# The order of sixteen matmuls per weight tile in a two-layer block with expert tables: interleaved, or in runs

## The chip, the cores and the metric

One core of a Trainium2 chip runs the whole program in one launch. The metric is the device time of that core in microseconds. The kernel before took 2291.82 us, the median of three runs (2289.64 to 2294.68).

## The reference, cut to what matters

The program is a retention and attention block with a feed-forward part, and after it two layers that each end in an expert layer over 16,384 experts. The change touches only products of 256 tokens with the weights of these expert layers:

```
def peer(h, wq, keys, u_tab, v_tab):                    # 256 tokens h, once in each of 2 layers
    q = (h @ wq)                                        # 1024 -> 2048: the queries
    s = einsum(q, keys)                                 # 128 keys per half
    ... top 16 of each half, top 16 of their sums: idx, gate = softmax(best)
    act = gelu(einsum('nd,nhkd->nhk', h, u_tab[idx]))   # the kernel forms h @ u_tab.T for all 16384
    return einsum('nhk,nhkd->nd', gate * act, v_tab[idx])
```

The reference gathers 16 rows of the tables for each token and head. The kernel computes the product with the whole first table (16,384 x 1024), and later multiplies the whole second table with a weight matrix that is zero where no expert was chosen.

## The kernel before, in words

**Numbers in two parts.** Weights come as 32-bit floats and are used at the matmul's reduced 32-bit format (fp32r). For accuracy each weight tile is split: `spl` is the rounded, high part, which ScalarE makes (L1097); `low` is what is left, `ring - spl`, which VectorE makes (L2600), or GpSimd for every second tile of the first 64 of the table (L2921, rule `lo_on_dve`). The tokens are split in the same way: `hT[:, 0]` is their high part, `hT[:, 1]` their low part. A product is then three: high by high, high weight by low token, low weight by high token.

**A weight tile.** Tiles have 128 x 1024 words, 512 KB. Five slots (`SLOTS`) hold the raw tile, its high and its low part. SyncE loads tile n when TensorE has told that it is done with tile n - 5 (`used`). ScalarE makes the high part two or three tiles ahead of its use, VectorE or GpSimd the low part behind it.

**The order written out by hand.** There is no scheduler: every engine has its own program, and semaphores with counted events join them. `hi.at(n)` is the event "the high part of tile n is there", `lo_at(n)` the same of the low part. `pe_take` waits for the low part, which is made from the high one, and so for both.

**Token-minor products.** In the expert layer 16 query tiles (`pe_peer`, loop over f) and 128 tiles of the first table (`pe_u`, 64 pairs) have the same form: 8 blocks k of 128 inputs. The stationary operand is a 128 x 128 piece of the weights. For the high part of the weights one matmul of 512 columns takes both parts of the tokens as moving operand (256 tokens high, 256 low, two pieces of `hT` that do not lie side by side) and fills one PSUM bank. For the low part one matmul of 256 columns takes the high tokens and adds to the first half of that bank. `mm3_both` writes these two for one block, wide then narrow; for the last block the narrow one goes first, so that the matmul that ends the group covers the whole bank. That makes 16 matmuls per tile, 16 + 128 tiles per layer, 288 tiles in both. The whole bank is read by ScalarE and VectorE when the tile (or the pair) is done.

**The first query tile.** The tokens' low part comes from VectorE in steps: events `("lo", k)`, where blocks 2 and 3, 4 and 5, 6 and 7 come in pairs from one instruction (L2447). Only the tile f = 0 waits for them, block by block.

**What stands between the tiles.** After f = 11 and f = 15 TensorE computes 32 small score products (L2804), after the pairs 14 and 30 of the table it transposes the chosen experts (L2815), and in the second half of the table each pair is preceded by 16 small matmuls that scatter the gates (`pe_scatter`, L2864). After that come 128 tiles of the second table (`pe_v`), with `mm3`: 12 matmuls of 512 columns per tile (L450 to L452), whose moving operand is the weight tile.

Of the kernel before, what the change touches and what calls it, by code (L numbers as in the profile page):

```python
# [174 lines left out]
U_BANK = (1, 4, 6)  # L175
# [254 lines left out]
def cut(p, f):  # L430
    return f(p[0]), f(p[1])
# [3 lines left out]
    return v[:, tb, c * 512:(c + 1) * 512]  # L435


def mm3_both(q, b, l, r, start, stop):


    if not stop:
        q.matmul(b[:, :].rearrange("p (z t) -> p z t", z=2), l[0], r, start=start, stop=False)  # L442
        return q.matmul(b[:, 0:256], l[1], r[:, 0], start=False, stop=False)  # L443
    q.matmul(b[:, 0:256], l[1], r[:, 0], start=False, stop=False)  # L444
    return q.matmul(b[:, :].rearrange("p (z t) -> p z t", z=2), l[0], r, start=False, stop=True)  # L445


def mm3(q, o, l, r, start, stop):
# [52 lines left out]
def pe_take(q, P, n):  # L501
    q.wait_ge(*P.lo_at(n))
    return P.tile(n)
# [1065 lines left out]
def ln_out(act, dve, tb, c):  # L1569

    return (act if c else dve).at(("ln", tb, c))
# [1202 lines left out]
def pe_peer(q, P, l):  # L2774
    T = T_PEER[l]
    b4act, b4dve = P.stage(("abo", "pool")[l])[1:]
    pe, act, dve = P.stage(f"peer{l}")
    if l == 0:
        first = [b4act.at(("turn", g)) for g in (4, 5, 2, 3)]
    else:  # L2780
        first = [b4dve.at(("mTf", 2)), b4dve.at(("mTf", 3)), b4act.at(("e", 5)), b4act.at(("e", 7))]
    pe_turns(q, P, pe, (0, 1, 2, 3),
             lambda k, tb: (P.xr[:, tb, k * 128:(k + 1) * 128], ln_out(b4act, b4dve, tb, k // 4)), first)
    for f in range(16):
        n = T + f
        sl = pe_take(q, P, n)
        if f == 0:
            q.wait_ge(*act.at(("turn", 3)))
        elif f == 2:
            q.wait_ge(*act.at(("turn", 7)))  # L2790
        elif f % 2 == 0:
            q.wait_ge(*dve.at(("q", f // 2 - 2)))
        for k in range(8):
            if f == 0:
                q.wait_ge(*dve.at(("lo", k)))
            t = mm3_both(q, P.ps[f % 4], cut(sl, lambda v: v[:, k * 128:(k + 1) * 128]), P.hT[:, :, k, :],
                         k == 0, k == 7)
        t.then_inc(*pe.mark(("used", n), *([("q", f // 2)] if f % 2 else [])))
        for tb, g0 in SC_AFTER.get(f, ()):
            q.wait_ge(*P.line(f"keys{g0 // 8}_loaded").at((l, g0 // 8)))  # L2800
            q.wait_ge(*dve.at(("q", g0 // 2 + 1)))
            q.wait_ge(*(act.at(("sc", tb, g0 - 8)) if g0 >= 8 else b4dve.at(("y", tb, g0 // 4))))
            for g in range(4):
                t = q.matmul(P.ps[4 + 2 * tb + g0 // 4 % 2][:, g * 128:(g + 1) * 128],  # L2804
                             P.qT[:, g0 + g, tb * 128:(tb + 1) * 128],
                             P.keys[:, (g0 + g) * 128:(g0 + g + 1) * 128], start=True, stop=True)
            t.then_inc(*pe.mark(("sc", tb, g0)))
    for p in range(32):
        pe_u(q, P, l, p)
        if p % 16 == 14:  # L2810
            tb = p // 16
            q.wait_ge(*dve.at(("gsoft", tb)))
            q.wait_ge(*(dve.at(("rtout", 0)) if tb else dve.at(("q", 6))))
            for z in range(3):
                t = q.transpose(P.ps[0][:, z * 128:(z + 1) * 128], P.ij[:, z, :], P.ident[:, :])  # L2815
            t.then_inc(*pe.mark(("rt", tb)))
    for r in range(32):
        pe_scatter(q, P, l, 0, r)
        pe_u(q, P, l, 32 + r)
    for r in range(32):  # L2820
        pe_scatter(q, P, l, 1, r)
        pe_v(q, P, l, 2 * r)
        pe_v(q, P, l, 2 * r + 1)
    for j in range(64, 125):
        pe_v(q, P, l, j)
        pe_fold(q, P, ("v", l, j))
    for tb in range(2):
        for c in range(2):
            for j in range(125, 128):
                pe_v(q, P, l, j, (tb,), (c,))  # L2830


def pe_u(q, P, l, p):

    pe, act, dve = P.stage(f"peer{l}")
    if p >= 3:
        q.wait_ge(*dve.at(("us", p - 3)))
    elif p:
        q.wait_ge(*act.at(("sc", p - 1, 12)))
    else:  # L2840
        q.wait_ge(*dve.at(("q", 7)))
    for d in range(2):
        n = T_PEER[l] + 16 + 2 * p + d
        sl = pe_take(q, P, n)
        for k in range(8):
            t = mm3_both(q, P.ps[U_BANK[p % 3] + d], cut(sl, lambda v: v[:, k * 128:(k + 1) * 128]),
                         P.hT[:, :, k, :], k == 0, k == 7)
        t.then_inc(*pe.mark(("used", n), *([("u", p)] if d else [])))


# [35 lines left out]
def pe_program(q, P):  # L2886
    pe_in(q, P)
    pe_wo(q, P)
    pe_up(q, P)
    pe_down(q, P)  # L2890
    pe_ab(q, P)
    pe_abo(q, P)
    pe_peer(q, P, 0)
    pe_pool(q, P)
    pe_peer(q, P, 1)
# [256 lines left out]
```

## Time and profile before

| | |
|---|---|
| median of three runs | 2291.82 us |
| the profiled execution | 2289.48 us, of which the span of the instructions is 2288.2 us |
| TensorE busy (matmuls) | 2237.6 us, 98% of the span |
| wide matmuls of the touched tiles, L442 | 2016, mean 401 ns |
| narrow matmuls of the touched tiles, L443 | 2016, mean 281 ns |
| VectorE, ScalarE, GpSimd busy | 82%, 52%, 7% |
| mean granted TensorE clock | 0.993 of full |

How to read it: matmuls are pipelined, and the time that the profile gives to one of them reaches from its start to the modelled arrival of its results, so that the times of neighbours overlap. What a matmul costs in a stream is the distance from its start to the start of the next one, and this is read from the times in the left column of the timeline. L444 and L445 are the two matmuls of the last block, narrow and wide; there are 288 of each.

### The profile page before, as it was taken

How to read it: one execution, taken by the hardware profiler on the slowest of the kernel's cores; microseconds unless marked ns; L12 is line 12 of the kernel's file. 1: busy time of each engine (PE TensorE's matmuls, PEld its weight loads, DVE VectorE, ACT ScalarE, POOL GpSimd, SP SyncE). 2: the span in 40 equal slices, each digit the busy share in tenths (PEclk: the TensorE clock that was granted, in tenths of full speed). 3: DMA queues.
4: the chain of work that ended last, by engine and by line, in shares of the span. 5: the costliest groups of instructions: out<-in, count | busy, mean ns of one | idle time of the engine just before them, and what ended most of it. 6: DMA issues, size and time to landing. Idle time of an engine off the chain costs nothing.

```text
span 2288.2 us, 34776 instructions
## 1 busy us (share of the span) xinstructions
PE 2237.6 (98%) x13446; PEld 1887.6 (82%) x13446; DVE 1868.9 (82%) x3365; ACT 1199.7 (52%) x1754; POOL 168.4 (7%) x75
## 2 busy tenths in 40 slices
PE   9999999999999999999999999899999999999997
PEld 7789978777888888888888877788888888887886
DVE  8679996568688988888888888869998888887656
ACT  7555554456456555554444445455665554444553
POOL 0000000000044400000000000014430000000000
PEclk9999999999999999999999999999999999999999
DMA  8366593233555555555558996455555555556674
GB/s 293 123 207 218 192 356 114 92 120 102 184 176 185 188 175 169 172 170 175 175 175 300 340 357 235 147 185 185 185 185 173 173 171 173 175 175 217 218 239 136
DMA packets 123508, 442.32 MB, mean 193 GB/s; under 512 B 13760, under 2 KB 16832, under 8 KB 122704
## 3 DMA queue, kind: packets, MB, share of 16 engines
q1 hardware_dynamic: 117464, 425.04, 56.4%
q10 hardware_dynamic: 5880, 15.06, 1.9%
q8 instruction: 108, 1.77, 0.3%
q14 instruction: 56, 0.46, 0.1%
HBM read 436.88 MB, written 3.16 MB: 192 GB/s over the span
## 4 chain that ended last, share of the span: by engine, by line
PE 82%; DVE 10%; ACT 3%; DMA 2%; issue 2%; SPq 0%; ACTq 0%; DVEq 0%
PE psum L442 21%; PE psum L450 13%; PE psum L452 13%; PE psum L451 13%; PE psum L443 10%; PE psum L445 3%; PE psum L2864 3%; DVE low L2600 3%; DVE acc L1777 2%; PE psum L444 1%; DVE cv L2108 1%; DMA ring<-in_peer_v 1%; ACT spl L1097 1%; ACT cv L1398 1%; PE psum L918 1%
## 5 line engine op out<-in xcount | busy, mean ns | idle before, releaser
L2600 DVE TENSOR_TENSOR low<-ring,spl 128x1024 fp32r<-128x1024 f32 x638 | 779.2, 1228 | 255.0 <-ACT spl L1097 253.4
L1097 ACT ACTIVATE spl<-ring 128x1024 fp32r<-128x1024 f32 x702 | 735.4, 1053 | 288.2 <-DMA ring<-in_peer_u 163.7
L442 PE MATMUL psum<-hT,spl 128*128 128x512 f32 x2016 | 730.7, 401 | 2.5 <-DVE hT L1757 2.5
L443 PE MATMUL psum<-hT,low 128*128 128x256 f32 x2016 | 566.5, 281 | 0.0
L442 PEld LDWEIGHTS psum<-hT,spl 128*128 128x128 f32 x2016 | 381.2, 189 | 81.2 <-issue 3.1
L450 PE MATMUL psum<-spl,Ws 128*128 128x512 f32 x1024 | 407.0, 398 | 7.0 <-DVE Ws L2638 7.0
L452 PE MATMUL psum<-spl,Ws 128*128 128x512 f32 x1024 | 399.6, 390 | 0.0
L451 PE MATMUL psum<-low,Ws 128*128 128x512 f32 x1024 | 398.3, 389 | 0.0
L443 PEld LDWEIGHTS psum<-hT,low 128*128 128x128 f32 x2016 | 382.8, 190 | 9.6
L1706 ACT ACTIVATE Ws<-S 128x256 fp32r<-128x256 f32 x256 | 106.6, 417 | 357.0 <-PE psum L452 352.4
L2921 POOL TENSOR_TENSOR low<-ring,spl 128x1024 fp32r<-128x1024 f32 x64 | 162.0, 2532 | 1135.6 <-ACT spl L1097 1135.6
L450 PEld LDWEIGHTS psum<-spl,Ws 128*128 128x128 f32 x1024 | 192.4, 188 | 47.5 <-DVE low L2600 9.0
L452 PEld LDWEIGHTS psum<-spl,Ws 128*128 128x128 f32 x1024 | 192.2, 188 | 41.6
L451 PEld LDWEIGHTS psum<-low,Ws 128*128 128x128 f32 x1024 | 192.6, 188 | 38.8 <-issue 0.7
L1689 ACT ACTIVATE S<-psum 128x512 f32<-128x512 f32 x128 | 76.5, 598 | 152.1 <-PE psum L445 151.9
L2633 DVE TENSOR_TENSOR S<-psum,S 128x512 f32<-128x512 f32 x128 | 87.7, 685 | 48.6 <-ACT S L1689 48.3
L450 PE MATMUL psum<-spl,hT 128*128 128x512 f32 (+1 forms) x284 | 115.4, 406 | 7.2 <-DVE low L2600 4.9
L445 PE MATMUL psum<-hT,spl 128*128 128x512 f32 x288 | 114.4, 397 | 0.0
L452 PE MATMUL psum<-spl,hT 128*128 128x512 f32 (+1 forms) x284 | 111.0, 391 | 0.0
L451 PE MATMUL psum<-low,hT 128*128 128x512 f32 (+1 forms) x284 | 110.7, 390 | 0.0
L2638 DVE TENSOR_TENSOR Ws<-S,Ws 128x256 fp32r<-128x256 f32 x256 | 106.6, 417 | 1.1 <-ACT Ws L1706 1.1
L450 PE MATMUL psum<-hT,spl 128*128 128x256 f32 x352 | 102.6, 291 | 3.8 <-DVE low L2600 2.1
(413 smaller groups left out, 3038.1 us busy)
## 6 DMA issues: line engine op xcount, KB each, us to landing
ring<-in_peer_u SPq DMA_DIRECT2D x256, 512.0 KB, 3.5
ring<-in_peer_v SPq DMA_DIRECT2D x256, 512.0 KB, 3.7
vring<-in_ada_w SPq DMA_DIRECT2D x56, 512.0 KB, 6.2
ring<-in_w_up SPq DMA_DIRECT2D x44, 512.0 KB, 5.2
aring<-in_ada_w SPq DMA_DIRECT2D x40, 512.0 KB, 5.2
ring<-in_ab_in SPq DMA_DIRECT2D x32, 512.0 KB, 3.5
ring<-in_peer_wq SPq DMA_DIRECT2D x32, 512.0 KB, 4.3
ring<-in_w_down SPq DMA_DIRECT2D x22, 512.0 KB, 5.9
```

Of the source, the lines that this page charges most:

```text
L442: q.matmul(b[:, :].rearrange("p (z t) -> p z t", z=2), l[0], r, start=start, stop=False)
L443: return q.matmul(b[:, 0:256], l[1], r[:, 0], start=False, stop=False)
L445: return q.matmul(b[:, :].rearrange("p (z t) -> p z t", z=2), l[0], r, start=False, stop=True)
L450: q.matmul(o, l[0], r[0], start=start, stop=False)
L451: q.matmul(o, l[0], r[1], start=False, stop=False)
L452: return q.matmul(o, l[1], r[0], start=False, stop=stop)
L1097: q.activation(P.spl[:, m % SLOTS, 0:w], P.ring[:, m % SLOTS, 0:w], ACT.Copy).then_inc(*P.hi.mark(m))
L1706: q.activation(P.Ws[:, j % 3, 0, :], P.S[:, j, :], ACT.Copy).then_inc(*act.mark(("ws", j)))
L2600: q.tensor_tensor(P.low[:, n % SLOTS, 0:w], P.ring[:, n % SLOTS, 0:w], P.spl[:, n % SLOTS, 0:w].bitcast(F32), ALU.subtract).then_inc(*P.lo ...
L2633: q.tensor_tensor(x, P.psum[:, b:b + 2, 0:256], x, ALU.add).then_inc(*dve.mark(("us", p)))
L2638: q.tensor_tensor(P.Ws[:, j % 3, 1, :], P.S[:, j, :], P.Ws[:, j % 3, 0, :].bitcast(F32), ALU.subtract).then_inc(*dve.mark(("ws", j)))
L2921: q.tensor_tensor(P.low[:, n % SLOTS, 0:w], P.ring[:, n % SLOTS, 0:w], P.spl[:, n % SLOTS, 0:w].bitcast(F32), ALU.subtract).then_inc(*P.lo ...
```

## The change

`mm3_both` goes. A new function, `pe_tokens`, writes a tile's sixteen matmuls: the wide ones of blocks 0 to 6, then the narrow ones of all eight blocks, then the wide one of block 7, which ends the group. At the tile's start it waits for the high part only, and for the low part ahead of the first narrow matmul. For f = 0 the waits for the tokens' low part stand ahead of the wide matmul of each block; the one of block 7 stands ahead of the narrow ones.

```diff
-def mm3_both(q, b, l, r, start, stop):
-    if not stop:
-        q.matmul(b[:, :].rearrange("p (z t) -> p z t", z=2), l[0], r, start=start, stop=False)
-        return q.matmul(b[:, 0:256], l[1], r[:, 0], start=False, stop=False)
-    q.matmul(b[:, 0:256], l[1], r[:, 0], start=False, stop=False)
-    return q.matmul(b[:, :].rearrange("p (z t) -> p z t", z=2), l[0], r, start=False, stop=True)
+def pe_tokens(q, P, b, n, x_hi):
+    hi, lo = P.tile(n)
+    w = lambda v, k: v[:, k * 128:(k + 1) * 128]
+    wide = b[:, :].rearrange("p (z t) -> p z t", z=2)
+    q.wait_ge(*P.hi.at(n))
+    for k in range(7):
+        x_hi(k)
+        q.matmul(wide, w(hi, k), P.hT[:, :, k, :], start=k == 0, stop=False)
+    x_hi(7)
+    q.wait_ge(*P.lo_at(n))
+    for k in range(8):
+        q.matmul(b[:, 0:256], w(lo, k), P.hT[:, 0, k, :], start=False, stop=False)
+    return q.matmul(wide, w(hi, 7), P.hT[:, :, 7, :], start=False, stop=True)
...
-        for k in range(8):
-            if f == 0:
-                q.wait_ge(*dve.at(("lo", k)))
-            t = mm3_both(q, P.ps[f % 4], cut(sl, lambda v: v[:, k * 128:(k + 1) * 128]), P.hT[:, :, k, :],
-                         k == 0, k == 7)
+        t = pe_tokens(q, P, P.ps[f % 4], n, lambda k: q.wait_ge(*dve.at(("lo", k))) if f == 0 else None)
...
-            t = mm3_both(q, P.ps[U_BANK[p % 3] + d], cut(sl, lambda v: v[:, k * 128:(k + 1) * 128]),
-                         P.hT[:, :, k, :], k == 0, k == 7)
+        t = pe_tokens(q, P, P.ps[U_BANK[p % 3] + d], n, lambda k: None)
```

TensorE's program around the border between two tiles of the first table, before (L442 and L445 wide, L443 and L444 narrow; `s_split_lo_pool` is GpSimd's event for a low part, `s_peer0_dve` the one by which VectorE gives a PSUM bank back):

```order
L442 MATMUL psum<-hT,spl 128x512
L443 MATMUL psum<-hT,low 128x256
L444 MATMUL psum<-hT,low 128x256
L445 MATMUL psum<-hT,spl 128x512
L442 MATMUL psum<-hT,spl 128x512 [waits s_split_lo_pool,s_peer0_dve]
L443 MATMUL psum<-hT,low 128x256
L442 MATMUL psum<-hT,spl 128x512
```

The same place of the changed kernel, a whole tile with its neighbours' ends (L447 and L452 wide, L451 narrow):

```order
L451 MATMUL psum<-hT,low 128x256 [waits s_split_lo_dve]
L451 MATMUL psum<-hT,low 128x256 x7
L452 MATMUL psum<-hT,spl 128x512
L447 MATMUL psum<-hT,spl 128x512 [waits s_split_hi,s_peer0_dve]
L447 MATMUL psum<-hT,spl 128x512 x6
L451 MATMUL psum<-hT,low 128x256 [waits s_split_lo_pool]
L451 MATMUL psum<-hT,low 128x256 x7
L452 MATMUL psum<-hT,spl 128x512
```

The narrow matmuls, which stood one by one behind the wide ones, now stand in one row of eight; the wide ones stand in a row of eight across the border of two tiles; and the wait for the low part has moved from the tile's first matmul to its eighth.

TensorE's program at the first query tile of layer 0, before:

```order
L442 MATMUL psum<-hT,spl 128x512 [waits s_peer0_dve,s_peer0_act,s_split_lo_dve]
L443 MATMUL psum<-hT,low 128x256
L442 MATMUL psum<-hT,spl 128x512 [waits s_peer0_dve]
L443 MATMUL psum<-hT,low 128x256
L442 MATMUL psum<-hT,spl 128x512 [waits s_peer0_dve]
```

And now:

```order
L447 MATMUL psum<-hT,spl 128x512 [waits s_peer0_dve,s_split_hi,s_peer0_act]
L447 MATMUL psum<-hT,spl 128x512 [waits s_peer0_dve] x6
L451 MATMUL psum<-hT,low 128x256 [waits s_split_lo_dve,s_peer0_dve]
L451 MATMUL psum<-hT,low 128x256 x7
```

Here `s_peer0_dve` is the event of the tokens' low part: the six waits of blocks 1 to 6 now follow each other at the distance of one wide matmul instead of a wide and a narrow one.

## Rows read from the trace of the kernel before

**Rows 1.** The page: engines (busy us, share, instructions) and the wide matmuls (busy, mean, idle before)
```profile
PE 2237.6 (98%) x13446; PEld 1887.6 (82%) x13446; DVE 1868.9 (82%) x3365; ACT 1199.7 (52%) x1754; POOL 168.4 (7%) x75
...
L442 PE MATMUL psum<-hT,spl 128*128 128x512 f32 x2016 | 730.7, 401 | 2.5 <-DVE hT L1757 2.5
```
**Rows 2.** Two stretches inside the expert layers: length, busy us per engine, clock, DMA
```profile
600.00:1200.00 600.00, 600.00 (x4016) 510.42 (x4015) 512.38 (x1035) 316.14 (x412) 81.09 (x32) 1.00 0.56 177
1500.00:2000.00 500.00, 500.00 (x3382) 429.81 (x3381) 431.67 (x901) 271.76 (x348) 80.89 (x32) 1.00 0.57 178
```
**Rows 3.** TensorE's waits for a low part, whole span: us in total, times, longest
```profile
PE psum L450 <- DVE low L2600: 8.5, 20, 1.4
```
**Rows 4.** Timeline, VectorE then TensorE: the shortest lead of a low part
```profile
617.03 1.23 DVE L2600 TENSOR_TENSOR low<-ring,spl 128x1024 fp32r<-128x1024 f32 x1 [2.85 <-ACT spl L1097]
...
619.03 0.40 PE L442 MATMUL psum<-hT,spl 128*128 128x512 f32 x1
```
**Rows 5.** Timeline of TensorE, one tile of the first table; the last row 20 tiles later
```profile
651.40 0.40 PE L442 MATMUL psum<-hT,spl 128*128 128x512 f32 x1
651.63 0.28 PE L443 MATMUL psum<-hT,low 128*128 128x256 f32 x1
651.75 0.40 PE L442 MATMUL psum<-hT,spl 128*128 128x512 f32 x1
...
653.99 0.40 PE L445 MATMUL psum<-hT,spl 128*128 128x512 f32 x1
654.22 0.40 PE L442 MATMUL psum<-hT,spl 128*128 128x512 f32 x1
...
707.80 0.40 PE L442 MATMUL psum<-hT,spl 128*128 128x512 f32 x1
```
**Rows 6.** Timeline of TensorE, an unbroken run of wide matmuls (attention output, L450 to L452)
```profile
573.08 0.39 PE L452 MATMUL psum<-spl,MT 128*128 128x512 f32 x1
...
579.20 0.39 PE L452 MATMUL psum<-spl,MT 128*128 128x512 f32 x1
```
**Rows 7.** Timeline of TensorE, an unbroken run of narrow matmuls (feed-forward part)
```profile
182.16 0.28 PE L450 MATMUL psum<-hT,spl 128*128 128x256 f32 x1
...
183.60 0.28 PE L450 MATMUL psum<-hT,spl 128*128 128x256 f32 x1
```
**Rows 8.** Timeline of TensorE, wide matmuls right behind a scatter (second table)
```profile
1189.49 0.47 PE L450 MATMUL psum<-spl,Ws 128*128 128x512 f32 x1
1189.81 0.39 PE L451 MATMUL psum<-low,Ws 128*128 128x512 f32 x1
...
1192.11 0.39 PE L452 MATMUL psum<-spl,Ws 128*128 128x512 f32 x1
```
**Rows 9.** Timeline of TensorE, two tiles behind a scatter, each to the next tile's start
```profile
902.30 0.48 PE L442 MATMUL psum<-hT,spl 128*128 128x512 f32 x1
...
905.21 0.40 PE L442 MATMUL psum<-hT,spl 128*128 128x512 f32 x1
...
1794.44 0.47 PE L442 MATMUL psum<-hT,spl 128*128 128x512 f32 x1
...
1797.30 0.40 PE L442 MATMUL psum<-hT,spl 128*128 128x512 f32 x1
```
**Rows 10.** Timeline, first query tile of layer 0, with VectorE's hT; last row: second tile
```profile
585.81 0.76 PE L442 MATMUL psum<-hT,spl 128*128 128x512 f32 x1 [1.07 <-DVE hT L1757]
586.21 0.69 DVE L2447 TENSOR_TENSOR hT<-yy_abo,hT 128x512 fp32r<-128x512 f32 x1
586.37 0.41 PE L443 MATMUL psum<-hT,low 128*128 128x256 f32 x1
...
587.01 0.41 PE L443 MATMUL psum<-hT,low 128*128 128x256 f32 x1
...
588.33 0.69 DVE L2447 TENSOR_TENSOR hT<-yy_abo,hT 128x512 fp32r<-128x512 f32 x1
...
590.87 0.40 PE L442 MATMUL psum<-hT,spl 128*128 128x512 f32 x1
```

More of the change, by code:

```diff
@@ L2785, in pe_peer @@
         n = T + f
-        sl = pe_take(q, P, n)
         if f == 0:
@@ L2843, in pe_u @@
         n = T_PEER[l] + 16 + 2 * p + d
-        sl = pe_take(q, P, n)
-        for k in range(8):
-            t = mm3_both(q, P.ps[U_BANK[p % 3] + d], cut(sl, lambda v: v[:, k * 128:(k + 1) * 128]),
-                         P.hT[:, :, k, :], k == 0, k == 7)
+        t = pe_tokens(q, P, P.ps[U_BANK[p % 3] + d], n, lambda k: None)
         t.then_inc(*pe.mark(("used", n), *([("u", p)] if d else [])))
```

## The prediction

> **What bounds the kernel now.** I read the engines' busy times first. TensorE is busy for 98% of the span, VectorE for 82% [rows 1]. The table by stretches then shows that inside the two expert layers TensorE is never idle: 600.00 of 600.00 us and 500.00 of 500.00, at a granted clock of 1.00, while VectorE is at 85% and the DMA engines at 56% [rows 2]. So in the stretches that the change touches the time is the number of matmuls times the distance between their starts, and nothing else. The third view, TensorE's waits, says the same from the other side: L442, the wide matmuls of the touched tiles, are kept waiting 2.5 us in all, for the tokens [rows 1]; every wait for a low part that the trace has stands at L450, in other stages [rows 3].
>
> That leaves the distances, which the timeline gives. A tile of the first table takes 651.40 to 654.22, 2.82 us, and 20 tiles take 707.80 - 651.40 = 56.40 us, again 2.820 each [rows 5]. Inside it a wide matmul is followed after 0.23 us (651.40 to 651.63) and a narrow one after 0.12 (to 651.75). With 0.119 for a narrow one, 8 x 0.119 = 0.95, the eight wide ones have 1.87 left, 0.234 each. The 288 tiles make some 812 us, a third of the span, so one per cent of them is 8 us.
>
> **What is removed and added, part by part.** The matmuls are the same: 8 of 512 and 8 of 256 columns per tile, with the same operands and as many weight loads. Only their neighbours differ. Before, 14 of 16 distances lie between matmuls of different width; now there are two changes of width per tile, and the rest are runs of eight.
>
> *Wide in a run.* The touched tiles have no run of wide matmuls, so I take bounds from other stages. A run that nothing disturbs goes from 573.08 to 579.20 in 27 steps, 0.2267 us each, and it crosses borders between weight tiles, with their waits, on the way [rows 6]. Right behind a scatter the steps from 1189.81 to 1192.11 are 10 in 2.30 us, 0.230 each [rows 8]. The upper bound is a wide one in the touched tiles themselves: 0.234 on average, and the only pair of wide neighbours there, L445 to L442, stands at 653.99 and 654.22, 0.23 [rows 5]. I take 0.2267, the long run's value, and add 0.008 at each of the two changes of width in a tile (0.234 - 0.2267), since a run of eight is short.
>
> *Narrow in a run.* From 182.16 to 183.60 there are 12 steps, 0.120 each [rows 7]. In the touched tiles the step shown is 0.12 as well, to the hundredth [rows 5], so anything from 0.115 to 0.125. I take 0.120, the run's.
>
> *The sum of a tile.* 8 x 0.2267 + 8 x 0.120 + 2 x 0.008 = 1.814 + 0.960 + 0.016 = 2.79 us, against 2.82: 0.03 less. It holds for the tiles that follow another tile. 74 of the 288 do not: 64 follow a scatter, 4 the scores, 4 a transpose, 2 are the first of their layer. 214 x 0.03 = 6.4 us less.
>
> *Tiles behind small matmuls.* They took 2.91 us in layer 0 (902.30 to 905.21) and 2.86 in layer 1 (1794.44 to 1797.30) [rows 9]. Now: the first wide matmul 0.32, as in 1189.49 to 1189.81 [rows 8], seven at 0.230, eight narrow at 0.120, in all 2.89. That lies between the two, and I put the 72 at nothing, with bounds of -1.4 us (72 x 0.02) and +2.2 (72 x 0.03).
>
> *The first query tile.* This is where the new order costs something. VectorE gives the low tokens of two blocks with each L2447: from 586.21 + 0.69 = 586.90 to 588.33 + 0.69 = 589.02, one every 1.06 us. TensorE asks for them once in two blocks. One block, a wide and a narrow matmul, takes 587.01 - 586.37 = 0.64 us here, at the low clock; by their columns 0.427 and 0.213 [rows 10]. So a pair of blocks took 1.28 us, more than VectorE needs, and nothing waited. Now a pair takes 2 x 0.427 = 0.85, less than 1.06. Block 6 would start at 585.81 + 0.56 + 5 x 0.427 = 588.50 and has to wait until 589.02: 0.5 us, which the narrow matmuls behind it can't fill any more, since they stand last. In two layers 1.0 us is added.
>
> *The separate waits.* The low part with the shortest lead that I found was ready at 617.03 + 1.23 = 618.26, its tile began at 619.03 [rows 4]. Since low parts are early by 0.8 us and more, a wait that comes 7 x 0.23 = 1.6 us later gives nothing. The wait for the high part costs nothing either: it is earlier still, and in the run of rows 6 waits at the borders leave no mark. Behind a waiting matmul all of TensorE's program would queue, but no wait of these is ever open. Cover gone: if low parts came 1 us later, the new order would hide it and the old would not; the change buys slack here, no time.
>
> *What it triggers.* A tile that is 1% shorter asks the loads for 1% more, at a DMA share of 0.56, and VectorE for 1% more, at 85% [rows 2]. Neither becomes the bound.
>
> The sum: -6.4 + 1.0 = -5.4 us on the profiled execution's 2289.48 us (span 2288.2 and 1.3 around it): 2284.1. This execution lies 2.3 us below the median of the runs, 2291.82, and I predict the median: 2286.4.
>
> **A rule that speaks against a gain.** By the rows the distance depends on the neighbours: 0.234 for a wide matmul among narrow ones, 0.2267 in a run [rows 5, 6]. The Trainium skill, page "TensorE: Matmul & The Clock Gate", section "Back-to-back issue gap", states a gap that follows from a matmul's own columns alone, N / 2.4 + 2.5 ns when warm, 216 ns for 512 and 109 for 256. By that rule a tile would take 8 x 0.216 + 8 x 0.109 = 2.60 us in either order, an estimate from the page, and the change would move nothing; the trace has 2.82, so part of the distance is outside the rule, and whether that part is for each matmul or for each change of width is the question.
>
> **The rivals.**
>
> *A. No change.* The surplus is a property of the place and not of the change of width: wide matmuls in the new runs keep what they have behind a disturbance, 0.230 [rows 8], or a little over, and the narrow ones go up from 0.119 to 0.120. A tile is 8 x 0.231 + 0.96 = 2.81, 0.01 less; 214 x 0.01 = 2.1 us against 1.0 added: 2290.7. For it: rows 8 need ten wide matmuls to come down to 0.2267, and a run here has eight. Against it: a tile without scatter has no 16 short matmuls to recover from.
>
> *B. Slower.* The two pieces of `hT` that a wide matmul reads don't lie side by side, while the runs of rows 6 and 8 read one piece; if this is what costs the 0.007, it stays, and the narrow ones lose what they had between wide ones. 8 x 0.235 + 8 x 0.122 = 2.856, 0.036 more for 214 tiles, 7.7 us, and 1.0 for the first tiles: 2300.5. It decides from a tile of 2.84 us on. For it: the border pair L445 to L442 is no faster than the others. Against it: behind a scatter the same matmuls do a tile in 0.32 + 2.54 = 2.86 [rows 9], that is 15 steps with 0.2267 and 0.120 almost exactly (7 x 0.2267 + 8 x 0.120 = 2.55), with the same two pieces.
>
> *C. More.* Narrow matmuls keep 0.115 in a run and the tiles behind a scatter gain too: 8 x 0.2267 + 8 x 0.115 = 2.73; 214 x 0.09 = 19 less, 72 x 0.02 = 1.4 less: 2272. Rows 7 speak against it. A half of it is 2281.
>
> *D. The separate waits do what they say,* and tiles start earlier because they no longer wait for the low part. There is no such wait in the trace to remove [rows 3]; this gives no change, and is part of A.
>
> *E. The clock.* The first tile runs at the low level; if the new stalls of 0.51 us kept it there for another tile, it would cost about as much as the first: 590.87 - 585.81 = 5.06 us [rows 10] against 2.82, 2.2 us per layer, 4.4 in all, and 2290.8 with the gain.
>
> **How the numbers follow.** My forecast has a chance of 0.50, A with D 0.27, B 0.11, C 0.05, E 0.07. Measurement can't tell less than 0.2%, 4.6 us, from no change: this calls for under 2287.2 for faster and over 2296.4 for slower. My forecast's own spread, some 3 us, crosses the first bound, and so 0.12 of its 0.50 goes to "no change". Faster: 0.38 + 0.05 + a little of A, 0.02, and of E, 0.01 = 0.46; slower: B's 0.09 and 0.03 of the rest = 0.12; no change: 0.42. The likeliest case gives 2286.4. The range goes from 2280 (half of C) to 2295 (between A and B).
>
> **What would show it.** Timeline after: the distance between starts in the run of L447 is 0.227 where I am right, 0.231 for A, 0.235 for B; of L451 0.120; a tile of the first table takes 2.79, 2.81 or 2.86. At the first query tile the wide matmuls of blocks 2, 4 and 6 start late, 0.5 us in all by block 6, in either layer. No wait of L451 for L2600 anywhere. I'm wrong if the tile has not moved from 2.82, or if the time moves by more than 5 us in stages that the change does not touch.

## The result, and the profile after

The changed kernel takes 2286.13 us (median of 15 runs, 2283.75 to 2290.14), the kernel before, timed beside it, 2290.72 (15 runs, 2287.15 to 2294.72). The ratio is 0.9983, with an interval of 0.9976 to 0.9990: 4.6 us less, where 5.4 less were forecast, and 2286.4 us as the time. The interval leaves out 1, but the gain lies at the edge of what a measurement of this kernel can tell from no change. The kernel before alone had medians of 2291.51 us (32 runs) and 2287.81 us (21 runs) in two later measurements. So a time below is compared with the kernel before timed beside it, and small differences are read from the tiles in the traces.

Most line numbers have moved by 7: L2607 is what L2600 was (VectorE makes a low part), L457 to L459 were L450 to L452, L2454 was L2447. The scatter, L2864, is now L2863. The page of the kernel after, TensorE and the two kinds of matmul of the touched tiles (busy us, mean ns of one, idle before them):

```profile
PE 2233.5 (98%) x13446; PEld 1889.3 (83%) x13446; DVE 1864.8 (82%) x3365; ACT 1201.4 (53%) x1754; POOL 168.5 (7%) x75
...
L447 PE MATMUL psum<-hT,spl 128*128 128x512 f32 x2016 | 520.0, 397 | 2.5 <-ACT yy_abo L1454 1.4
...
L451 PE MATMUL psum<-hT,low 128*128 128x256 f32 x2304 | 322.5, 283 | 0.0
```

The number of matmuls is that of [rows 1], TensorE's busy time 4.1 us less. The idle time before L447, 2.5 us, is what it was, and the narrow ones wait for nothing. The busy us of a line are no measure here: L442 had 730.7 and L447 has 520.0 for as many matmuls, since overlapping neighbours of one line are now counted together. What has to be read is the distance between starts. The two stretches of [rows 2] in the kernel after (length, then PE, PEld, DVE, ACT, POOL, clock, DMA):

```profile
600.00:1200.00 600.00, 600.00 (x4046) 514.44 (x4045) 513.82 (x1040) 318.48 (x414) 81.64 (x32) 1.00 0.57 178
1500.00:2000.00 500.00, 500.00 (x3400) 432.62 (x3400) 431.46 (x902) 273.55 (x350) 80.42 (x32) 1.00 0.56 178
```

TensorE still never idles, at the same clock: it now starts 4046 matmuls in the same 600 us instead of 4016, and 3400 instead of 3382. That is the gain, seen from afar. The timeline of TensorE shows it from near, one tile of the first table with its neighbours' ends (start us, us, then xcount: consecutive ones are put together):

```profile
651.21 1.77 PE L447 MATMUL psum<-hT,spl 128*128 128x512 f32 x7
652.82 1.11 PE L451 MATMUL psum<-hT,low 128*128 128x256 f32 x8
653.77 0.40 PE L452 MATMUL psum<-hT,spl 128*128 128x512 f32 x1
654.00 0.40 PE L447 MATMUL psum<-hT,spl 128*128 128x512 f32 x1
```

The tile takes 654.00 - 651.21 = 2.79 us, as forecast, against 2.82 in [rows 5]. Over 20 tiles it is 2.793. On average over the 212 tiles that nothing disturbs, the starts are, in ns, 236, 228, 233, 231, 227, 227, 227 apart for the wide ones of the run, then 113, 119 and six times 120 for the narrow ones, then 233 for the closing wide one. A tile behind a scatter:

```profile
831.75 0.64 PE L2863 MATMUL psum<-Bb,Ab 128*128 128x64 f16 x16
832.23 1.84 PE L447 MATMUL psum<-hT,spl 128*128 128x512 f32 x7
833.90 1.12 PE L451 MATMUL psum<-hT,low 128*128 128x256 f32 x8
834.86 0.40 PE L452 MATMUL psum<-hT,spl 128*128 128x512 f32 x1
835.09 0.40 PE L447 MATMUL psum<-hT,spl 128*128 128x512 f32 x1
```

It takes 2.86 us in both layers, where [rows 9] had 2.91 and 2.86. And the first query tile of layer 0 with the second one behind it:

```profile
584.70 4.11 PE L447 MATMUL psum<-hT,spl 128*128 128x512 f32 x7 [1.43 <-ACT yy_abo L1454]
588.61 1.91 PE L451 MATMUL psum<-hT,low 128*128 128x256 f32 x8
590.32 0.63 PE L452 MATMUL psum<-hT,spl 128*128 128x512 f32 x1
590.74 2.00 PE L447 MATMUL psum<-hT,spl 128*128 128x512 f32 x7
592.59 1.10 PE L451 MATMUL psum<-hT,low 128*128 128x256 f32 x8
593.52 0.40 PE L452 MATMUL psum<-hT,spl 128*128 128x512 f32 x1
593.76 0.62 PE L447 MATMUL psum<-hT,spl 128*128 128x512 f32 x2
```

The first takes 6.04 us (590.74 - 584.70) against 5.06 in [rows 10], the second 3.02. TensorE's waits for a low part, whole span (us, times, longest), now stand at the line that was L450, as in [rows 3]; there is none at L451:

```profile
PE psum L457 <- DVE low L2607: 9.1, 21, 1.4
```

*Where the time went, profiled execution against profiled execution* (span 2284.3 against 2288.2, 3.8 us less before rounding). The 212 tiles that nothing disturbs gave 2.8 us in layer 0 (2819.3 to 2793.3 ns each) and 1.8 in layer 1 (2810.7 to 2793.3), together -4.6. The 72 behind small matmuls gave 1.2 in layer 0 and took 0.3 in layer 1: -0.9. The first two tiles of a layer took 1.2 more in layer 0 and 0.2 in layer 1: +1.4. The rest of the program took 0.3 more. The same sum over the other traces says that this is no accident of two executions: the 288 tiles take 820.1, 821.3 and 820.2 us in the three traces with the old order throughout (before, its second trace, old order with the waits apart), and 816.0, 814.4 and 814.9 in the three with the new one (after, one wait, and first tile old, which has the old order in one tile per layer).

One number in this list does not fit the theory of the prediction: in layer 1 the tiles of the kernel before averaged 2810.7 ns and not 2820. Its trace has a second kind of tile, which the prediction overlooked. TensorE's timeline of the kernel before, in the second half of layer 1's first table, from the start of a tile to the small matmuls behind it:

```profile
1717.65 0.40 PE L442 MATMUL psum<-hT,spl 128*128 128x512 f32 x1
...
1720.20 0.40 PE L445 MATMUL psum<-hT,spl 128*128 128x512 f32 x1
1720.44 0.35 PE L2864 MATMUL psum<-Bb,Ab 128*128 128x64 f16 x6
```

This tile is in the old order and takes 2.79 us. In [rows 5] a wide and a narrow matmul take 353 ns together; here they take 347, as much as 227 + 120 (a wide one is followed after 230 ns, a narrow one after 117). The whole of this half runs so, and its tiles behind a scatter take 2.86 instead of 2.90. So the old order can be as fast as the new one, and a fixed cost per change of width can't be the cause. But the fast kind stands only in this half, where a scatter comes after every second tile. Among the query tiles and in the first half of the table, where up to 31 tiles follow each other undisturbed, the old order is back at 2.82 within two tiles of each disturbance, in both layers. The experiments were made to settle what that means.

### The profile page after: what moved, and what is told of

Its sections match the earlier page's. It is cut to its first block, busy times and chain, and to the rows that moved or that the text cites. A ratio compares the mean times of both kernels' runs of the same rounds, so it can differ in the third digit from the quotient of the medians.

```text
span 2284.3 us, 34778 instructions
## 1 busy us (share of the span) xinstructions
PE 2233.5 (98%) x13446; PEld 1889.3 (83%) x13446; DVE 1864.8 (82%) x3365; ACT 1201.4 (53%) x1754; POOL 168.5 (7%) x75
## 3 DMA queue, kind: packets, MB, share of 16 engines
HBM read 436.88 MB, written 3.16 MB: 193 GB/s over the span
## 4 chain that ended last, share of the span: by engine, by line
PE 82%; DVE 10%; ACT 3%; DMA 3%; issue 2%; SPq 0%; ACTq 0%; DVEq 0%
PE psum L447 21%; PE psum L457 13%; PE psum L459 13%; PE psum L458 13%; PE psum L451 12%; PE psum L452 3%; PE psum L2863 3%; DVE low L2607 3%; DVE acc L1784 2%; DMA ring<-in_peer_v 2%; DVE cv L2115 1%; ACT spl L1104 1%; ACT cv L1405 1%; PE psum L925 1%; PE psum L2806 1%
## 5 line engine op out<-in xcount | busy, mean ns | idle before, releaser
L2607 DVE TENSOR_TENSOR low<-ring,spl 128x1024 fp32r<-128x1024 f32 x638 | 778.7, 1228 | 259.3 <-ACT spl L1104 258.8
L447 PE MATMUL psum<-hT,spl 128*128 128x512 f32 x2016 | 520.0, 397 | 2.5 <-ACT yy_abo L1454 1.4
L447 PEld LDWEIGHTS psum<-hT,spl 128*128 128x128 f32 x2016 | 375.5, 189 | 76.7 <-DVE hT L2454 3.6
L457 PE MATMUL psum<-spl,Ws 128*128 128x512 f32 x1024 | 407.1, 398 | 6.9 <-DVE Ws L2645 6.8
L459 PE MATMUL psum<-spl,Ws 128*128 128x512 f32 x1024 | 399.5, 390 | 0.0
L458 PE MATMUL psum<-low,Ws 128*128 128x512 f32 x1024 | 398.4, 389 | 0.0
L451 PEld LDWEIGHTS psum<-hT,low 128*128 128x128 f32 x2304 | 315.7, 191 | 22.6
L451 PE MATMUL psum<-hT,low 128*128 128x256 f32 x2304 | 322.5, 283 | 0.0
L457 PEld LDWEIGHTS psum<-spl,Ws 128*128 128x128 f32 x1024 | 192.4, 188 | 48.0 <-DVE low L2607 9.7
L459 PEld LDWEIGHTS psum<-spl,Ws 128*128 128x128 f32 x1024 | 192.1, 188 | 41.4
L458 PEld LDWEIGHTS psum<-low,Ws 128*128 128x128 f32 x1024 | 192.6, 188 | 38.7 <-issue 0.7
L457 PE MATMUL psum<-spl,hT 128*128 128x512 f32 (+1 forms) x284 | 116.0, 409 | 7.7 <-DVE low L2607 5.5
L452 PE MATMUL psum<-hT,spl 128*128 128x512 f32 x288 | 114.0, 396 | 0.0
L459 PE MATMUL psum<-spl,hT 128*128 128x512 f32 (+1 forms) x284 | 111.4, 392 | 0.0
L458 PE MATMUL psum<-low,hT 128*128 128x512 f32 (+1 forms) x284 | 111.3, 392 | 0.0
L457 PE MATMUL psum<-hT,spl 128*128 128x256 f32 x352 | 102.5, 291 | 3.9 <-DVE low L2607 2.2
```

The lines of the kernel that those rows point to most:

```text
L447: q.matmul(wide, w(hi, k), P.hT[:, :, k, :], start=k == 0, stop=False)
L451: q.matmul(b[:, 0:256], w(lo, k), P.hT[:, 0, k, :], start=False, stop=False)
L452: return q.matmul(wide, w(hi, 7), P.hT[:, :, 7, :], start=False, stop=True)
L457: q.matmul(o, l[0], r[0], start=start, stop=False)
L458: q.matmul(o, l[0], r[1], start=False, stop=False)
L459: return q.matmul(o, l[1], r[0], start=False, stop=stop)
```

## The experiments

In what follows W is a wide matmul (512 columns), N a narrow one (256). The kernel before has WN seven times and then NW; the kernel after seven W, eight N, W.

**Only one wait.** The new order, with one wait for the low part at the tile's start, as before.

```diff
-    q.wait_ge(*P.hi.at(n))
+    q.wait_ge(*P.lo_at(n))
...
-    q.wait_ge(*P.lo_at(n))
```

> The order of the changed kernel (seven wide, eight narrow, one wide), but one wait per tile, for the low part, at its start, as before. Theory 1, the order alone gives the gain: a tile that follows a tile stays at 2.793 us, and the time is that of the changed kernel, 2286 us, 0.998 of before. Theory 2, the separate waits give it: the tile goes back to 2.81 or 2.82 and the time to 2290 to 2291.

Measured: 2286.15 us, ratio 0.9980 (0.9971 to 0.9989) to the kernel before. TensorE's timeline of this kernel:

```profile
706.98 1.77 PE L447 MATMUL psum<-hT,spl 128*128 128x512 f32 x7
708.59 1.11 PE L450 MATMUL psum<-hT,low 128*128 128x256 f32 x8
709.54 0.40 PE L451 MATMUL psum<-hT,spl 128*128 128x512 f32 x1
709.77 0.40 PE L447 MATMUL psum<-hT,spl 128*128 128x512 f32 x1
```

The tile is 2.79 us without the separate waits: they are worth nothing here.

**Only the waits.** The old order, with the two waits apart (`pe_tokens` writes its matmuls by a string, in this and in the later kernels).

```diff
+    order = 'WNWNWNWNWNWNWNNW'
```

> The order of before (wide and narrow in turn), with the waits of the changed kernel: the high part at the tile's start, the low part ahead of the first narrow matmul. Theory 1, the order: a tile stays at 2.820 us in layer 0, time 2290.7 as before, ratio 1.000 within 0.001. Theory 2, the waits: 2.79 and 2286.

Measured: 2291.08 us, ratio 0.9997 (0.9988 to 1.0006). The waits alone do nothing, from this side too. What the trace adds is the second kind of tile, in the other layer than in the trace of before: here the second half of layer 0's first table runs at 2.793 us, all other stretches at 2.82 on average. TensorE's timeline (L459 wide; the first row of each tile holds the wide one before it as well):

```profile
836.43 0.63 PE L459 MATMUL psum<-hT,spl 128*128 128x512 f32 x2
...
839.22 0.40 PE L459 MATMUL psum<-hT,spl 128*128 128x512 f32 x1
...
1721.69 0.63 PE L459 MATMUL psum<-hT,spl 128*128 128x512 f32 x2
...
1724.51 0.39 PE L459 MATMUL psum<-hT,spl 128*128 128x512 f32 x1
```

From closing wide to closing wide it is 839.22 - 836.43 = 2.79 in layer 0, and 1724.51 - 1721.69 = 2.82 in layer 1.

**The kernel before once more**, unchanged, one run, to see whether the kind of tile belongs to a stretch of the program.

> The kernel before, profiled once more. In its first trace the undisturbed tiles took 2.820 us nearly everywhere, but 2.793 in the second half of the first table of layer 1; with only the waits changed it was 2.793 in layer 0 and 2.820 in layer 1. Theory 3, the order in turn has two steady patterns and an execution falls into one or the other, stretch by stretch: again only these two values, 2.793 and 2.820, but not in the same stretches. Rival, the stretch sets it (its other work): 2.793 in the second half of layer 1 and only there.

Measured: the undisturbed tiles of every stretch average between 2.818 (layer 1's queries) and 2.820 us; both second halves are at 2819.9 ns, their tiles behind scatters at 2902.8. The second half of layer 1, which ran at 2.793 in the first trace, is slow here. The same program shows either pattern at the same place: it is the execution's, not the stretch's. In the three traces with the old order two of six second halves are fast, and no other stretch is. The time, a single one, was 2293.0, 1.2 us over the 2291.82 of the first runs; its span is 3.5 us longer than that of the first trace, of which the tiles have 1.2, and 2.1 had passed before the first of them began.

**Strict turns.** WN eight times: sixteen changes of width in a tile.

```diff
+    order = 'WNWNWNWNWNWNWNWN'
```

> The changed kernel's waits, but wide and narrow strictly in turn in all eight blocks, the narrow one of block 7 closing the tile: no two of a width stand side by side at the border. Theory 1 (each change of width costs): the slowest of all, 16 changes, 2.82 us per tile or more. Theory 3 (a change of width costs nothing, the surplus of 0.020 comes from the border's two wide or two narrow matmuls, and 0.047 from the slow pattern): 2.773 to 2.78 in the fast pattern, 8 x 0.3533 = 2.827 in the slow one.

Measured, one run: 2284.13 us, with the kernel before at 2293.08 beside it. TensorE's timeline of a tile of layer 0, and of tiles of layer 1 on both sides of a transpose (L458 wide, L455 narrow, L2824 the transpose; the wide rows are starts of tiles):

```profile
711.58 0.39 PE L458 MATMUL psum<-hT,spl 128*128 128x512 f32 x1
711.81 0.28 PE L455 MATMUL psum<-hT,low 128*128 128x256 f32 x1
...
714.35 0.39 PE L458 MATMUL psum<-hT,spl 128*128 128x512 f32 x1
...
1600.67 0.39 PE L458 MATMUL psum<-hT,spl 128*128 128x512 f32 x1
...
1603.44 0.39 PE L458 MATMUL psum<-hT,spl 128*128 128x512 f32 x1
...
1606.22 0.49 PE L2824 MATMUL psum<-ident,ij 128*128 128x128 f32 x3
...
1609.37 0.40 PE L458 MATMUL psum<-hT,spl 128*128 128x512 f32 x1
...
1612.20 0.40 PE L458 MATMUL psum<-hT,spl 128*128 128x512 f32 x1
```

The tile of layer 0 takes 2.77 us, as much as 8 x 0.2267 + 8 x 0.120 = 2.773 with no surplus at all (its steps are 230 and 117 ns), and so does the one of layer 1 ahead of the transpose (1600.67 to 1603.44). Behind the transpose a tile takes 2.83 (1609.37 to 1612.20). With sixteen changes of width a tile can be faster than the new order's 2.793, which has two. The theory of the prediction falls with this row. Strict turns have two steady patterns, 2.773 and 2.827 on average, and fall into either. The pattern changes only where small matmuls stand between two tiles (scores, a transpose, a scatter); in a stretch that nothing disturbs, it stays.

**Strict turns, timed.** The same kernel in 11 runs.

> The order strictly in turn again, another execution, and timed. In its first trace the tiles took 2.773 us in the first half of the table of layer 0, 2.80 on average in that of layer 1, 2.778 in both second halves, and up to 2.83 among the query tiles. Theory 3, two steady patterns that an execution falls into: other stretches are at 2.83 now, and the runs spread between about 2281 and 2291; ratio 0.996 to 0.999. Theory 4, the program decides it: the same stretches at the same values.

Measured: 2289.68 us (2282.27 to 2293.61), ratio 1.0002 (0.9993 to 1.0011), less than the gain that was expected. The lowest of these runs, 2282.27, was the profiled one. In its trace the slow pattern stands in other places than above (in layer 0 the second part of the table's first half is slow here and was fast there), but both second halves are at 2.778 again, and the 288 tiles take 813.9 us, after 812.1 in the first trace: less than any trace of the new order. Over many executions strict turns still give what the kernel before gives. Whether the slow pattern filled the other ten runs, no trace shows; that they are no faster stays open.

The spread of the times, 11.3 us, says nothing on the patterns, since the kernel before beside them has 10.1 in 21 runs. A part of it goes with the mean granted clock of a run: here 2282.27 at 0.995, 2286.32 to 2290.60 at 0.993, 2289.85 to 2293.61 at 0.992.

**Two widths between.** Runs of four (WWWWNNNNWWWNNNNW) and of two (WWNNWWNNWWNNWNNW), one run each.

```diff
+    order = 'WWWWNNNNWWWNNNNW'
```

> The changed kernel with runs of four: W4 N4 W3 N4 W1 (W wide, N narrow), so two runs of each width per tile instead of one. Theory 1, the surplus over 2.773 is 0.021 for each way from narrow to wide and back (the run of eight costs 0.029 in its first five wide matmuls and gives 0.008 back in the first narrow one): 2.773 + 2 x 0.02 = 2.80 to 2.815 us. Theory 3, one surplus of 0.020 per tile whatever the runs: 2.793.

Measured: 2286.21 us. TensorE's timeline, from the closing wide one of one tile, counted with the next run of four, over two tiles:

```profile
706.63 1.32 PE L459 MATMUL psum<-hT,spl 128*128 128x512 f32 x5
...
709.43 1.31 PE L459 MATMUL psum<-hT,spl 128*128 128x512 f32 x5
...
712.22 0.39 PE L459 MATMUL psum<-hT,spl 128*128 128x512 f32 x1
```

Two tiles take 5.59 us, 2.797 each by the mean of the stretch; in the second half of the table it is 2.810, and 2.887 behind a scatter.

```diff
+    order = 'WWNNWWNNWWNNWNNW'
```

> The changed kernel with runs of two: W2 N2 W2 N2 W2 N2 W1 N2 W1, four runs of each width. Theory 1: 4 x 0.01 to 0.02 over 2.773, 2.81 to 2.85 us per tile. Theory 3: 2.793, or 2.82 where the slow pattern takes hold.

Measured: 2294.68 us, tiles of 2.813, in the second half 2.818. The time of a single run misleads here: this trace is 9.1 us longer than that of the changed kernel (2293.4 against 2284.3), and 5.7 of them lie before the first touched tile, which starts at 590.4 instead of 584.7 us. These two alone would have borne out a cost per change of width (2, 4 and 8 or so changes: 2.793, 2.797, 2.813); it is the strict turns that rule it out.

**The first query tile in the old order,** all else new.

```diff
+    order = 'WNWNWNWNWNWNWNNW' if first else 'WWWWWWWNNNNNNNNW'
```

> The changed kernel with the first query tile of each layer in the order of before. In the trace of the changed kernel the first two tiles of a layer take 6.04 + 3.01 us (layer 0) and 5.55 + 2.80 (layer 1), against 5.06 + 2.79 and 5.26 + 2.92 before. Theory 1, the stalls come from the low tokens' waits standing one wide matmul apart: the first tile goes back to 5.06 (5.26), and 0.5 to 1.4 us are saved over the changed kernel: about 2285, ratio 0.9975. Rival, the longer first tile comes from the clock level and not from the order: no difference in the first two tiles' sum, 2286.1.

Measured: 2285.48 us (2282.62 to 2290.53), ratio 0.9976 (0.9967 to 0.9986) to the kernel before. The first two tiles took 5.055 + 2.77 us in layer 0 and 5.287 + 3.16 in layer 1. The first tile is back at its old length, as in [rows 10]; the second one ran long in layer 1 because the clock rose later there. Over all traces the two tiles together take 7.24 to 8.45 us in the old order (mean of eight 7.87) and 7.68 to 9.05 in the new one (mean of six 8.32): some 0.45 us per layer, with a spread larger than that. It is the best median and the best ratio of all kernels here that leave nothing out; from the changed kernel's 0.9983 its interval can't tell it, nor from the 0.9980 of the one-wait kernel.

**Runs over a pair of tiles.** In the first table both tiles of a pair go together: 14 W, 16 N, 2 W.

```diff
...
     for d in range(2):
-        n = T_PEER[l] + 16 + 2 * p + d
-        t = pe_tokens(q, P, P.ps[U_BANK[p % 3] + d], n, lambda k: None)
-        t.then_inc(*pe.mark(("used", n), *([("u", p)] if d else [])))
+        q.wait_ge(*P.hi.at(n + d))
+        for k in range(7):
+            q.matmul(wides[d], w(P.tile(n + d)[0], k), P.hT[:, :, k, :], start=k == 0, stop=False)
+    for d in range(2):
+        q.wait_ge(*P.lo_at(n + d))
+        for k in range(8):
+            q.matmul(banks[d][:, 0:256], w(P.tile(n + d)[1], k), P.hT[:, 0, k, :], start=False, stop=False)
...
```

> The changed kernel, and in the first table the two tiles of a pair are written as one: fourteen wide, sixteen narrow, two wide matmuls, so a pair has two changes of width instead of four. Theory 1, what is above 8 x 0.2267 + 8 x 0.120 = 2.773 us in a tile (now 0.020) belongs to the changes of width: a pair takes 2 x 2.773 + 0.020 = 5.567 instead of 5.587, 0.01 less per tile, 256 tiles, 2.5 us at most: 2283.6 to 2284.5. Rival, it belongs to the border between tiles (waits, another bank): it stays at 2.793 per tile and 2286.1. A third way, the slot of the first tile of a pair comes free about 1.4 us later and loads or high parts come late: waits of TensorE for spl or low appear, and the time is above 2287.

Measured: 2288.98 us, ratio 0.9997 (0.9988 to 1.0006): the gain is gone. The time is that of the third way foreseen, but the waits are others. TensorE's timeline in the first half of the table:

```profile
680.26 3.35 PE L2851 MATMUL psum<-hT,spl 128*128 128x512 f32 x14
683.44 2.08 PE L2855 MATMUL psum<-hT,low 128*128 128x256 f32 x16
685.35 0.63 PE L2857 MATMUL psum<-hT,spl 128*128 128x512 f32 x2
685.82 0.39 PE L2851 MATMUL psum<-hT,spl 128*128 128x512 f32 x1
```

5.56 to 5.57 us for a pair, against 2 x 2.793 = 5.586: two changes of run give 0.02 us together, whether a tile or a pair lies between them. That is 0.6 us per layer gained here. It is lost in the second half, where the small matmuls of the scatters wait for VectorE, as TensorE's waits show (us, times, longest):

```profile
PE psum L2874 <- DVE Bb L2578: 3.0, 3, 1.0
```

The tiles of that half take 183.68 and 182.62 us in the two layers, against 181.04 each for the changed kernel: 4.2 us more. With 1.2 gained in the first halves that is 3.0 more, and the medians are 2.9 apart (2288.98 - 2286.13). That a pair's first bank is now handed over 16 matmuls later is my explanation for the later VectorE; no run took that alone.

**Both ideas together:** the first tile in turns, pair runs only where no scatter comes, strict turns in the second half.

```diff
+    order = "WNWNWNWNWNWNWNWN" if turns else "WWWWWWWNNNNNNNNW"
...
+    if p >= 28:
...
+            t = pe_tokens(q, P, P.ps[U_BANK[p % 3] + d], n, lambda k: None, p >= 32)
```

> The best of each stretch put together: the first query tile of a layer in turn (saves about 0.3 us per layer), query tiles as in the changed kernel, the first 28 pairs of the table with one run of each width per pair (2.783 instead of 2.793 us, 56 tiles per layer: 0.6 us), and the second half of the table, where a scatter stands ahead of every second tile, strictly in turn (2.778 and 2.861 instead of 2.793 and 2.864: 0.6 us per layer). In all 3.0 us less than the changed kernel: 2283, ratio 0.9966 to 0.9972. If the pattern in turn is the slow one after the scatter this time, second halves take 2.82 and 2.90 and it is 2286 or more. Rival, the low parts or the gates of the scatter come late behind the pairs, as in the kernel with pair runs throughout: single stalls of TensorE of about 1.1 us.

Measured: 2285.87 us (2280.68 to 2290.75), ratio 0.9991 (0.9980 to 1.0001), where 0.9966 to 0.9972 were expected. The second half ran at 2777.9 ns per undisturbed tile in layer 0 and at 2796.3 in layer 1 of the profiled execution. The second number is no slow pattern. It comes from one tile of 3.37 us, ahead of a scatter that waits for VectorE; the 31 others have 2.778:

```profile
1708.35 0.63 PE L2885 MATMUL psum<-Bb,Ab 128*128 128x64 f16 x16 [0.43 <-DVE Bb L2583]
```

One transpose waits too, 1.0 us for VectorE. Each order gave its stretch about what it was to give, 1.1 us per layer in all. The rival that was foreseen, VectorE late behind the pairs, took most of it back: the two waits lengthen their tiles by 1.8 us. Without the first two tiles of each layer, the tiles take 798.1 us here and 798.6 in the changed kernel. The kernel has the lowest single run of all that leave nothing out, 2280.68, but by its ratio it is no better than the changed kernel.

**Narrow matmuls of 128 columns.** This leaves out the low part's product for tokens 128 to 255.

```diff
-        q.matmul(b[:, 0:256], w(lo, k), P.hT[:, 0, k, :], start=False, stop=False)
+        q.matmul(b[:, 0:128], w(lo, k), P.hT[:, 0, k, 0:128], start=False, stop=False)
```

> The changed kernel with narrow matmuls of 128 instead of 256 columns: the low part of the weights is left out for the tokens 128 to 255. It asks what sets the 0.120 us of a narrow matmul in a run. If it is the matmul's own columns plus 0.013, the distance becomes 0.053 + 0.013 = 0.067 and a tile 2.37 us. If it is the load of the next 128 x 128 weights behind it, the distance stays near 0.120 and the tile at 2.79, and a narrow matmul could carry no less at the same price.

Measured, one run: 2272.57 us. TensorE's timeline:

```profile
705.72 1.78 PE L447 MATMUL psum<-hT,spl 128*128 128x512 f32 x7
707.34 1.01 PE L451 MATMUL psum<-hT,low 128*128 128x128 f32 x8
708.18 0.44 PE L452 MATMUL psum<-hT,spl 128*128 128x512 f32 x1
708.46 0.40 PE L447 MATMUL psum<-hT,spl 128*128 128x512 f32 x1
```

With half the columns only one step of the narrow run is short, the 59 ns from the first narrow matmul to the second; the next ones stay 110 to 114 ns apart, where 256 columns have 120. The wide ones give a part back: the closing one is followed after 283 ns instead of 233 (708.18 to 708.46), and the run behind it no longer settles at 227 but goes on at 224 to 236. A tile takes 2.747 us, 0.046 less, though 8 x 128 columns at 2.4 GHz would be 0.43 less. So something other than the columns sets the distance of the narrow ones, and each matmul has a weight load of 128 x 128 beside it: a run of narrow matmuls in the kernel is within 0.01 us per step of a limit that halving their work does not move. That it is the load is inferred, not isolated.

## Why the prediction was right, and where its reason was wrong

- *What bounds the kernel*: right. The starts per us of TensorE account for the time; all other engines are where they were.
- *Wide in a run, 0.2267, and narrow in a run, 0.120*: right. The new run settles at 227 and 120 ns. With it rival B falls: a wide matmul that reads `hT` in two pieces is no slower in a run than one that reads one piece. Rival A's 0.231 appears only in the first steps of the run, and C's 0.115 not at all (the one 113 is the first step after the wide ones).
- *Two changes of width at 0.008 each*: the sum, 2.79, came out, but this step failed, and that the sum came out in spite of it is luck. The 0.234 of a wide one rested on 0.119 for a narrow one, which no row shows to the thousandth: in the slow tiles the trace of before has 235 for a wide and 117 for a narrow one on average, so that the wide ones of the old order had 9 ns too much and the narrow ones 3 too little. The new tile's surplus over 2.773 is 20 ns: the first five wide steps behind the narrow ones (233, 236, 228, 233, 231) have some 28 ns too much, the first two narrow ones behind the wide 8 too little. That alone could still be a price of the changes; strict turns rule it out, where sixteen changes cost nothing or 54 ns, by the pattern. What the runs show in its place: an order in turns falls into one of two steady patterns, 2.82 or 2.79 for the old order, and the order in runs sat at 2.793 in each of the traces that has it throughout (after, one wait, first tile old). The change does not make a cost per change of width smaller; it takes away the slow pattern, which the old order had in every long stretch and in four of six second halves. What sets the pattern in an execution stays open.
- *214 tiles x 0.03 = 6.4 us*: mis-sized, 4.6 in the trace. In layer 1 some of the tiles of before were already at 2.793. Against a trace of before that is slow throughout, as its second one, 212 x 0.027 = 5.7 would go.
- *72 tiles behind small matmuls, nothing*: -0.9 us. The 2.91 of layer 0 and 2.86 of layer 1 in [rows 9] were the two patterns, which the prediction had before its eyes and put its 2.89 between. The change brings the 64 behind a scatter to 2.86 and the 8 behind scores or a transpose to 2.88 or 2.89.
- *The first query tile, +1.0*: right in kind, +1.4 in the trace and about 0.9 by the mean of all traces. How it comes about was not quite foreseen. VectorE and the weight loads of the kernel after, at that tile:

```profile
585.14 0.69 DVE L2454 TENSOR_TENSOR hT<-yy_abo,hT 128x512 fp32r<-128x512 f32 x1
...
585.89 0.50 PEld L447 LDWEIGHTS psum<-hT,spl 128*128 128x128 f32 x2 [0.69 <-DVE hT L2454]
...
586.96 0.50 PEld L447 LDWEIGHTS psum<-hT,spl 128*128 128x128 f32 x2 [0.57 <-DVE hT L2454]
...
588.02 0.28 PEld L447 LDWEIGHTS psum<-hT,spl 128*128 128x128 f32 x1 [0.56 <-DVE hT L2454]
```

The waits are where the prediction had them: the wide matmuls of blocks 2, 4 and 6 start at 585.89, 586.96 and 588.02, each right after VectorE (585.14 + 0.69 = 585.83 for the first), and block 6 is 0.6 us later than its columns would have it from this tile's start (584.70 + 0.56 + 5 x 0.427 = 587.40). What it did not have is the weight load. It stands behind the same wait as its matmul (585.89 again), so it is no longer hidden: from a matmul that waited to the next one it is some 594 ns, where the columns alone give 427 at this clock. Between blocks 2 and 6 VectorE's step of 1.06 us covers that (594 + 472 = 1066); behind block 6 it is 0.17 us on top. The rest is the clock, and rival E has its share: the closing wide matmul of the first tile was still followed after 427 ns instead of 233, and the second tile of layer 0 took 3.01 us instead of 2.79. The stretches of the kernel after that hold the first and the second tile (columns as above):

```profile
584.70:590.74 6.04, 6.04 (x16) 4.04 (x17) 5.94 (x11) 3.78 (x6) 0.00 (x0) 0.50 0.25 83
590.74:593.76 3.02, 3.02 (x18) 2.60 (x17) 1.30 (x2) 0.00 (x0) 0.00 (x0) 0.92 0.95 340
```

The second begins at a clock that is still low for a part of it (0.92), before it rises to the high level. Both together are 0.4 us in layer 0, and not the 2.2 of the rival. How much of the first two tiles' time is the low clock differs from one execution to the next (7.68 us in layer 0 of the one-wait kernel, 9.05 here, in the same order).
- *The separate waits, nothing*: right, and shown by two runs, one that has the order without them and one that has them without the order (D falls). The slack that they give was never drawn on.
- *The rule weighed*, the Trainium skill's "Back-to-back issue gap" (page "TensorE: Matmul & The Clock Gate"), has 216 and 109 ns for these widths. The section gives its formula for an isolated matmul and says that in a stream the weight load counts too, which the prediction left out; its figure there for 512 columns, 131 ns, is not what these traces have. In undisturbed runs this case's traces have 227 and 120, so 11 more for either. In that the sum over a tile doesn't depend on the changes of width, the rule is nearer to the traces than the prediction was: in the fast pattern of strict turns it is 8 x 0.2267 + 8 x 0.120 us, though the single steps are 230 and 117 ns. That the columns alone set a distance is not so in this case: half of them left the narrow ones at 110 to 114 ns. What the rule has no word for is the slow pattern, and that is where the gain came from.

## What to carry to other kernels

Where matmuls of two widths take turns and TensorE is full, measure the distance between starts over many tiles, in each stretch and in several executions, before you put a price on a neighbour: here one program ran at 2.82 or at 2.79 us per tile, and one trace showed both. An order in runs gave the same 2.793 in every trace and so was worth 0.2% of the kernel. Strict turns were faster in both of their traces and no faster when timed over 11 runs, so one profile doesn't price an order. Runs have a price where operands arrive late: work that could fill a wait stands last, and weight loads behind the same wait lie open.

## What was not expected of the hardware

- One program's alternating matmuls (512 and 256 columns, a weight load each) kept to 353 or to 347 ns per pair for whole stretches, and which of the two differed between executions at the same place. Strict turns had 2.83 or 2.77 us for eight pairs, and went from one to the other only where small matmuls stood between two tiles.
- Behind a run of narrow matmuls the first wide steps of a run are up to 9 ns too long (233, 236, 228, 233, 231) before they settle at 227.
- Matmuls of 128 columns with a weight load each did not get below 110 ns apart in a run, but for its first step (59 ns); 256 columns had 120.
- A matmul that waits takes its weight load with it: 594 ns from its start to the next one's instead of 427 at the low clock.
